# A 14-norm transformer kernel on one Trainium2 core: where a centred norm subtracts its mean, and where the square-root table is loaded

## The reference

```python
def rmsnorm(x, g):
    y = x * lax.rsqrt(jnp.mean(x * x, axis=-1, keepdims=True) + EPS)
    return y * g

def layer_norm(x, g, b):
    mu = jnp.mean(x, axis=-1, keepdims=True)
    var = jnp.mean(jnp.square(x - mu), axis=-1, keepdims=True)
    return (x - mu) * lax.rsqrt(var + LN_EPS) * g + b

# second block, each sublayer, latent and context alike
x = layer_norm(ALPHA * x + gate * y, ln_g, ln_b)
h = x * (1.0 + scale) + shift      # input of the next sublayer
```

## Time and profile before

| | |
|---|---|
| median of 3 runs | 2692.1 us (2691.15 to 2692.31) |
| profiled execution | 2694.41 us, its span 2692.6 us |
| TensorE, VectorE, ScalarE busy | 93%, 70%, 41% of the span |
| mean granted TensorE clock | 0.961 of full |
| table loads ahead of the square root (L1244) | 12, for 14 square roots |

### The profile page before, as it was taken

One profiled execution on the slowest core, in us unless ns is written; L12 is line 12 of the kernel. 1 busy time (PEld: TensorE's weight loads), 2 busy tenths in 40 slices (PEclk: granted clock), 3 DMA queues, 4 the chain that ended last, 5 costly groups with the idle time before them and its releaser, 6 DMA issues.

```text
span 2692.6 us, 39417 instructions
## 1 busy us (share of the span) xinstructions
PE 2494.2 (93%) x15494; PEld 2250.0 (84%) x15494; DVE 1889.5 (70%) x3654; ACT 1101.7 (41%) x1631; POOL 0.2 (0%) x4
## 2 busy tenths in 40 slices
PE   4998989789989998899999899999799999797997
PEld 3998889789979887688888798888798888676997
DVE  7877977788879975635555669887685344666666
ACT  3444564344453323624222562222552222545444
POOL 0000000000000000000000000000000000000000
PEclk8998999989989999999999899999899999798999
DMA  8875857768858752432322256666274332222553
GB/s 304 297 249 184 272 166 238 248 230 284 252 179 261 219 160 71 141 101 79 94 86 91 80 190 198 197 192 197 93 252 140 101 96 91 73 76 65 186 181 109
DMA packets 161096, 452.63 MB, mean 168 GB/s; under 512 B 17680, under 2 KB 21264, under 8 KB 160912
## 3 DMA queue, kind: packets, MB, share of 16 engines
q1 hardware_dynamic: 160912, 450.11, 51.7%
HBM read 448.99 MB, written 1.05 MB: 167 GB/s over the span
## 4 chain that ended last, share of the span: by engine, by line
PE 57%; DVE 7%; ACT 4%; issue 2%; DMA 0%; ACTq 0%; SPq 0%; DVEq 0%
PE PS L1012 18%; PE PS L1013 18%; PE PS L1014 18%; ACT whi L1221 2%; DVE wlo L1478 1%; DVE X L1578 1%; PE PS L1156 1%; DVE X L1576 1%; DVE RS L1545 1%; ACT NT L1275 1%; PE PS L1038 1%; ACT Uh L1271 0%; PE PS L1202 0%; PE PS L1040 0%; DVE X L1461 0%
## 5 line engine op out<-in xcount | busy, mean ns | idle before, releaser
L1478 DVE TENSOR_TENSOR wlo<-raw,whi 128x1024 fp32r<-128x1024 f32 x602 | 735.8, 1223 | 479.0 <-ACT whi L1221 476.2
L1012 PE MATMUL PS<-Uh,wlo 128*128 128x256 f32 (+1 forms) x2992 | 972.1, 325 | 66.6 <-DVE Ul L1582 30.5
L1013 PE MATMUL PS<-Ul,whi 128*128 128x256 f32 (+1 forms) x2992 | 954.2, 319 | 0.0
L1014 PE MATMUL PS<-Uh,whi 128*128 128x256 f32 (+1 forms) x2992 | 953.6, 319 | 0.0
L1221 ACT ACTIVATE whi<-raw 128x1024 fp32r<-128x1024 f32 x602 | 633.2, 1055 | 718.2 <-PE PS L1014 715.7
L1012 PEld LDWEIGHTS PS<-Uh,wlo 128*128 128x128 f32 x2992 | 581.6, 194 | 120.2 <-issue 45.2
L1013 PEld LDWEIGHTS PS<-Ul,whi 128*128 128x128 f32 x2992 | 584.0, 195 | 35.1 <-issue 0.2
L1014 PEld LDWEIGHTS PS<-Uh,whi 128*128 128x128 f32 x2992 | 583.3, 195 | 35.1
L1012 PE MATMUL PS<-Hh,wlo 128*128 128x256 f32 (+1 forms) x1616 | 519.2, 321 | 18.8 <-DVE RS L1548 10.5
L1013 PE MATMUL PS<-Hl,whi 128*128 128x256 f32 (+1 forms) x1616 | 514.7, 318 | 0.0
L1014 PE MATMUL PS<-Hh,whi 128*128 128x256 f32 (+1 forms) x1616 | 514.5, 318 | 0.0
(11 more groups left out here) (178 smaller groups left out, 1849.6 us busy)
## 6 DMA issues: line engine op xcount, KB each, us to landing
MODS<-in_mm SPq DMA_DIRECT2D x168, 256.0 KB, 3.8
SCR<-in_mm SPq DMA_DIRECT2D x168, 256.0 KB, 3.6
raw<-in_f0i SPq DMA_DIRECT2D x64, 512.0 KB, 4.0
raw<-in_f1i SPq DMA_DIRECT2D x56, 512.0 KB, 3.6
raw<-in_f2i SPq DMA_DIRECT2D x56, 512.0 KB, 3.6
SCR<-in_ma SPq DMA_DIRECT2D x88, 256.0 KB, 5.3
raw<-in_w1i SPq DMA_DIRECT2D x44, 512.0 KB, 4.4
raw<-in_w2i SPq DMA_DIRECT2D x44, 512.0 KB, 4.3
```

What stands on the lines that cost most here:

```text
L1012: e.matmul(o, ll, rh, start=start, stop=False)
L1013: e.matmul(o, lh, rl, start=False, stop=False)
L1014: return e.matmul(o, lh, rh, start=False, stop=stop)
L1478: e.tensor_tensor(wlo[:, w.n % RING, :], raw[:, w.n % RING, :], whi[:, w.n % RING, :].bitcast(F32), ALU.subtract).then_inc(s["wlo"].tell(w ...
```

## The change

1. `tally` puts one more item, `sqrt_table`: ACT takes the square root of one column of ones, in ACT's queue just ahead of the norm's first square. The compiler's load of the table moves there.
2. A centred norm subtracts the mean from X itself, before the scaling: `centre`, on two tiles at once, reads the sums in PSUM. The first pair's stands between `stat` and `root`; those of the other pairs stand behind the scaling of the pair before. The product L1548 and the subtraction L1578 go.
3. The sums' bank is held until the last `centre` instead of until `root`.
4. In the last norm the `centre` of pairs 2, 4 and 6 stand behind `root` and ahead of all eight scalings; each tile then has one DVE operation instead of two.

```diff
@@ tally
         self.tallies[r] = t
+        self.put("sqrt_table")
@@ tallied
         self.put("stat", n=t["n"], r=r, bank=t["bank"], centred=t["centred"], eps=eps)
+        if t["centred"]:
+            self.centre(t, 0)
         self.fill(min(fills[0] - 1, 1))
-        self.put("root", n=t["n"], r=r, bank=t["bank"], centred=t["centred"])
+        self.put("root", n=t["n"], r=r)
+        if not t["centred"]:
+            self.release(t)
+        self.fill(fills[0] - 2)
+        return t
+
+    def centre(self, t, k):
+        self.put("centre", n=t["n"], k=k, r=t["r"], bank=t["bank"])
+        if k == KT - 2:
+            self.release(t)
+
+    def release(self, t):
         b = t["bank"][0]
         self.held.discard(b)
         if self.turn % 8 == b:
             self.turn += 1
@@ norm_tiles
             self.put(what, st=site, k=k, n=t["n"], r=r, after=after, **fields)
+            if t["centred"] and k in (0, 2, 4):
+                self.centre(t, k + 2)
@@ schedule, the last norm
     t = p.tallied(LAT, 1e-5, (0, 0))
+    for k in (2, 4, 6):
+        p.centre(t, k)
@@ ACT
+                elif w.what == "sqrt_table":
+                    on.wait_ge(s["ones_set"], 0)
+                    e.activation(small[:, 216:217], ones[:, 0:1], ACT.Sqrt)
@@ DVE, root
                     e.reciprocal(rs, rs).then_inc(s["rstd"].tell(w.n), 1)
-                    if w.centred:
-                        on.wait_ge(s["rstd"], w.n)
-                        e.scalar_tensor_tensor(out=mr, in0=PS[:, b, 0:S], scalar=1.0 / D, in1=rs, op0=ALU.mult,
-                                               op1=ALU.mult).then_inc(s["mrs"].tell(w.n), 1)
-                        done_with(w.bank, "mrs", w.n)
+                elif w.what == "centre":
+                    x = X[:, w.k:w.k + 2, lo:hi]
+                    on.wait_ge(s["mean2"], w.n)
+                    e.scalar_tensor_tensor(out=x, in0=PS[:, b, 0:S].unsqueeze(1).broadcast_to([P, 2, S]), scalar=-1.0 / D,
+                                           in1=x, op0=ALU.mult, op1=ALU.add).then_inc(s["centred"].tell((w.n, w.k)), 1)
+                    done_with(w.bank, "centred", (w.n, w.k))
@@ DVE, the tiles
-                            on.wait_ge(s["mrs"], w.n)
-                            e.tensor_tensor(x, x, rs, ALU.mult).then_inc(s["normed"].tell((w.st, w.k, "x")), 1)
-                            on.wait_ge(s["normed"], (w.st, w.k, "x"))
-                            e.tensor_tensor(x, x, mr, ALU.subtract).then_inc(s["normed"].tell((w.st, w.k)), 1)
+                        if w.what == "ln":
+                            on.wait_ge(s["centred"], (w.n, w.k))
+                        on.wait_ge(s["rstd"], w.n)
+                        e.tensor_tensor(x, x, rs, ALU.mult).then_inc(s["normed"].tell((w.st, w.k)), 1)
@@ DVE, finish
-                    on.wait_ge(s["mrs"], w.n)
-                    e.tensor_tensor(x, x, RS[:, 0, 0, :], ALU.mult).then_inc(s["final_x"].tell((w.k, 0)), 1)
-                    on.wait_ge(s["final_x"], (w.k, 0))
-                    e.tensor_tensor(x, x, RS[:, 0, 1, :], ALU.subtract).then_inc(s["final_x"].tell((w.k, 1)), 1)
+                    on.wait_ge(s["centred"], (w.n, w.k - w.k % 2))
+                    on.wait_ge(s["rstd"], w.n)
+                    e.tensor_tensor(x, x, RS[:, 0, 0, :], ALU.mult).then_inc(s["final_x"].tell(w.k), 1)
```

More of the change, by code:

```diff
@@ L322, in tallied @@
             self.turn += 1
-        self.fill(fills[0] - 2)
-        return t
     def norm_tiles(self, what, site, t, r, fills, after, **fields):
@@ L818 @@
     "root2", "prob2", "turned2", "o_hi", "last_x",
-    "ones_set", "wlo", "modded", "coef", "folded", "var", "rstd", "mrs", "normed", "ulo", "product", "hlo", "acc", "angle", "padded",
+    "ones_set", "wlo", "modded", "coef", "folded", "var", "rstd", "centred", "normed", "ulo", "product", "hlo", "acc", "angle", "padded",
     "pooled", "roped1", "mapped", "y_lo", "masked", "weight1", "merged", "m_lo", "v_part", "v_stat", "v_normed", "mixed",
@@ L1426, in scalar @@
                     x = X[:, w.k, 0:S]
-                    on.wait_ge(s["final_x"], (w.k, 1))
+                    on.wait_ge(s["final_x"], w.k)
                     e.activation(x, x, ACT.Identity, scale=vec("lg", 40 + w.k), bias=vec("lb", 40 + w.k)).then_inc(
@@ L1541, in vector @@
                 elif w.what == "root":
-                    h = lo // S
-                    rs, mr = RS[:, h, 0, :], RS[:, h, 1, :]
+                    rs = RS[:, lo // S, 0, :]
                     on.wait_ge(s["std"], w.n)
                     e.reciprocal(rs, rs).then_inc(s["rstd"].tell(w.n), 1)
-                    if w.centred:
-                        on.wait_ge(s["rstd"], w.n)
-                        e.scalar_tensor_tensor(out=mr, in0=PS[:, b, 0:S], scalar=1.0 / D, in1=rs, op0=ALU.mult,
-                                               op1=ALU.mult).then_inc(s["mrs"].tell(w.n), 1)
-                        done_with(w.bank, "mrs", w.n)
+                elif w.what == "centre":
[4 more added lines that the diff above has]
+                    done_with(w.bank, "centred", (w.n, w.k))
                 elif w.what == "rms":
@@ L1569, in vector @@
                         x = X[:, w.k:w.k + 2, lo:hi]
[L1570 to L1574, removed]
-                            on.wait_ge(s["mrs"], w.n)
-                            e.tensor_tensor(x, x, rs, ALU.mult).then_inc(s["normed"].tell((w.st, w.k, "x")), 1)
-                            on.wait_ge(s["normed"], (w.st, w.k, "x"))
-                            e.tensor_tensor(x, x, mr, ALU.subtract).then_inc(s["normed"].tell((w.st, w.k)), 1)
+                        rs = RS[:, h, 0, :].unsqueeze(1).broadcast_to([P, 2, S])
+                        if w.what == "ln":
+                            on.wait_ge(s["centred"], (w.n, w.k))
+                        on.wait_ge(s["rstd"], w.n)
+                        e.tensor_tensor(x, x, rs, ALU.mult).then_inc(s["normed"].tell((w.st, w.k)), 1)
                     low = w.k if w.what == "ctxu" else w.k - 1
```

## The result

| | before | after |
|---|---|---|
| median, us | 2691.95 (4 runs, 2691.15 to 2692.31) | 2666.51 (4 runs, 2665.04 to 2667.89) |
| profiled execution, its span | 2694.41, 2692.6 | 2667.44, 2665.6 |
| mean granted clock | 0.961 | 0.963 |

The ratio is 0.9906 with an interval of 0.9894 to 0.9918: faster by 25.4 us, 0.94%. Forecast were 2673 and a range of 2665 to 2684.

What follows compares the result with a forecast made beforehand. TensorE, 93% busy, loses time to norms only where it waits on the ACT and DVE chain to the last `Ul`. Terms 4.6 + 0.9 + 2.5 + (2.5 + 3.3) + 3.8 + 1.7 = 19.3 us: 2692.1 to 2673, range 2665 to 2684.

Steps and rivals of the forecast that it cites:

- forecast: Whole kernel, likeliest case: the summed gains hold, 2667 to 2679 us; chance 0.62.
- more than forecast: Rival: a norm's low-clock stretch falls away or the last centre is nearer 0.68; up to 6 us more, 2667 or below; 0.08.
- The chain of l11: At l11, 1.61 up to the first `Uh` plus 2.16 over three pairs: 3.8 us, all on the path.
- The last norm: At the last norm, ACT's first tile comes later but tiles follow at 0.51 instead of 0.80: 1.7 us gained.
- The pair of the context norms: Context norms without the subtraction: pairs gain 0.72, 0.36, 0.36, 0.72; with 0.27, 2.5 us at c00, c02 and c10.
- The `mean2` of c01: At c01 the root behind the Silus loads the table again: `mean2` at 1504.8 instead of 1503.25.
- The bank's wait: The 10.5 us PE waits for L1548 lie ahead of a longer wait for the folded sums, so not worth 10.5.
- The table: A table load taken away is worth 0.49 us, not its 1.28; at c00 the gain is gone.
- l01 and l02 lie under twelve context tiles: nothing.: Latent norms l01 and l02: hidden under twelve context tiles, gain nothing.
- l00's cap: At l00, TensorE works through to a wait of only 1.21 at 1101.30: c00 and l00 give 4.6 us, not 5.8.
- the clock takes half of it: Rival: five more dense stretches at the low clock cost half their length, 10 us less gain, 2683; chance 0.17.
- c01: At c01 the second table load makes the reciprocal 1.7 late instead of 0.2; 0.9 us of gain is left.

Runs made afterwards that it cites:

- hold_only: Kernel before plus change 3 alone: the sums' banks of all ten centred norms held as long as in the change; 2691.58 us, ratio 1.0001.
- centre_only: Changed kernel without any early root; 2662.22 us, ratio 0.9894 to the kernel before.
- roots_only: Kernel before plus change 1 alone, the root of one column, norms as before; 2691.26 us, ratio 1.0002.
- centre_l01_l02: Kernel before with the mean taken first in norms l01 and l02 alone; 2688.19 us, ratio 0.9987.
- ctx_only: Kernel before with the mean taken first in context norms c00, c01, c02 and c10 alone, no roots; 2682.01 us, ratio 0.9968.
- after_again: The changed kernel, unaltered, timed once more in a later set; 2665.14 us, ratio 0.9901 to the kernel before.
- roots_late: Changed kernel with early roots only at l11 and the last norm, whose later centres each stand behind the scaling before; 2661.66 us, ratio 0.9888 to before.
- best2: roots_late with each context-norm centre right behind the accumulate of its fill's first tile; 2657.67 us, ratio 0.9874 to the kernel before.
- double: Changed kernel with a second DVE operation of the same size behind each centre; 2679.17 us, ratio 0.9955 to the kernel before.

## Why the prediction was right, and where it was off

**The number.** 2666.5 lies in the range of 2665 to 2684, by 1.5 us at its lower end. The case "forecast", 2667 to 2679 with 0.62, just missed it; it is the case "more than forecast", 2667 or below, that came true, and that had a chance of 0.08. That the number counts as right is partly luck: the sum was 19.3 us and the medians give 25.4.

**Right, by its own steps.** `centre` at 0.70 (684 ns). The chain of l11, 3.8 forecast and 3.58 measured; the first `Uh` 4.41 behind `mean2` instead of 2476.04 - 2469.91 = 6.13, so 1.72 earlier where 1.6 was forecast. The last norm, 1.7 and 1.59. The pair of the context norms: cycles of 5.70 and 5.99 after (1070.58 to 1076.57) against 6.36, where 6.0 was forecast, 2.5 a norm and 2.57 and 2.38 measured. The `mean2` of c01 at +1.5, 1.51 measured. l10's 3.3, 3.34. The bank's wait is nothing: shown by hold_only and by the folds' wait that took it over. The table: 0.49 where it isn't hidden, shown in l11, and hidden in the context norms, shown by centre_only. (By the 2.66 us for a switch that the Trainium skill gives in ScalarE: Activation LUTs, What ACT_TABLE_LOAD costs, roots_only would have gained some 1.9 at each of six norms, an estimate; the runs show 0.50 from `mean2` to the square root in l11 and nothing in the total. The load's 1283 ns agree, the drain isn't there.) One slip of counting: it is two of eight loads at centred norms that stay, not two of ten; L1264 has two after.

**The step that failed: "l01 and l02 lie under twelve context tiles: nothing."** It took for granted that TensorE, once it has the first tiles, is fed by the fill for as long as the norm lasts. Before, one pair of l01 takes 6.80 us on DVE, because two weight chunks pass through DVE and ACT in each:

```profile
1552.92 0.69 DVE L1576 TENSOR_TENSOR X<-X,RS 128x512 f32<-128x512 f32 x1
...
1556.44 1.23 DVE L1478 TENSOR_TENSOR wlo<-raw,whi 128x1024 fp32r<-128x1024 f32 x1 [1.77 <-ACT whi L1221]
...
1559.72 0.69 DVE L1576 TENSOR_TENSOR X<-X,RS 128x512 f32<-128x512 f32 x1
```

and TensorE has to wait for the first chunk of the pair that follows:

```profile
1564.52 0.39 PE L1012 MATMUL PS<-Uh,wlo 128*128 128x256 f32 x1 [0.78 <-DVE wlo L1478]
```

A second such wait follows in l01, 0.80, and l02 has two, 0.67 and 0.79. Such a wait costs more than it lists: the matmul ahead of it starts at 1563.46 and the one behind it at 1564.75, 1.29 for two steps that otherwise take 0.12 each, so 1.05 is lost. After, a pair takes 6.07 (scalings at 1544.12 and 1550.19), and no such wait is left. The count of matmuls (PE's busy time and, in brackets, their number) in the 30 us behind l01's `mean2` says the same: before, then centre_l01_l02. Behind l02's the counts are again 244 and 252, and hold_only has 244 behind l01's, so it isn't the bank.

```profile
1537.90:1567.90 30.00, 29.22 (x244) 29.01 (x243) 21.72 (x36) 22.39 (x37) 0.00 (x0) 1.00 0.39 125
```

```profile
1535.90:1565.90 30.00, 30.00 (x252) 30.00 (x251) 22.48 (x37) 25.70 (x43) 0.00 (x0) 1.00 0.44 141
```

So these norms were on the path, through `wlo` and not through `Ul`, and the weight chunks that queue behind the norm on DVE are what it held up. What they are worth can be read free of the clock if a part is ended where TensorE's own work begins or ends. From l01's `mean2` to the first matmul of the folded sums ahead of c02 it is 355.32 before, 355.33 in hold_only and 355.47 in ctx_only, but 353.27 in centre_l01_l02, 353.40 in centre_only and 353.26 after: 2.06, which is two waits of 1.05. From TensorE's first matmul of l02's fill to c10's `mean2` it is 356.53 before, 356.54 in hold_only and 356.53 in ctx_only, but 354.24 in centre_l01_l02 and 354.24 after: 2.29, two waits and a first matmul that ran at the low level before. So the norms that were put at nothing are worth some 4 us. (The 1.85 of l01 to c02 in the table is that 2.06 less 0.2: the work from the first of the sums to c02's `mean2` takes 5.68 before and 5.89 after, with a stretch at the low level in both, and 4.32 in hold_only and roots_only, where there is none.)

**l00's cap.** The 1.21 wait at 1101.30 made me stop l00's gain at 2.1; it is 3.40, all of the 3.3 that the same steps give without a cap. Between 1101 and 1116 the kernel before has four more waits of PE (0.33, 1.73, 1.09 and 0.64), for `wlo` and `Ul`; after, there are three in all of l00 (0.64, 1.10 and 1.13), none before 1105. So PE had room behind that wait too: the norm's chain set l00's length, and I had read one short wait as a limit without looking at those behind it.

**c02's 1.2 too much** is the rival "more than forecast", and so is the 0.9 that l02 to c10 gained beyond those 2.1. The granted clock at the end of c02's step, before, then ahead of that work in the changed kernel (PEclk is the third figure from the end):

```profile
1927.00:1934.00 7.00, 6.76 (x22) 5.48 (x23) 1.05 (x5) 5.26 (x11) 0.00 (x0) 0.53 0.09 36
```

```profile
1900.00:1912.00 12.00, 2.97 (x10) 2.61 (x11) 9.77 (x20) 7.74 (x15) 0.00 (x0) 0.57 0.30 87
```

Before, the low level, 1.2 GHz, still held while PE worked at the end of the norm; after, it falls on the stretch in which PE is idle (2.97 busy of 12) and is over when the work comes: from 1912 to 1921 the granted clock is 1.00. What that work takes at either level stands in the trace. The latent norm's sums are four pairs of matmuls that l02's `mean2` waits for; here are the first and the last pair, before, then after:

```profile
1929.89 1.05 PE L1038 MATMUL PS<-X,ones 128*128 128x256 f32 x2
...
1932.44 1.06 PE L1040 MATMUL PS<-SQ,ones 128*128 128x256 f32 x2
```

```profile
1917.58 0.59 PE L1055 MATMUL PS<-X,ones 128*128 128x256 f32 x2
...
1918.88 0.59 PE L1057 MATMUL PS<-SQ,ones 128*128 128x256 f32 x2
```

They take 3.61 us before and 1.89 after, 1.72 less. Before, `mean2` starts 0.04 behind them; after, it starts 0.96 behind them, because ACT is still at its Silu and that one's table load. So 0.80 of the 1.72 shows in c02 to l02. The other 0.92 shows in l02 to c10, where TensorE has begun the next sublayer 1.31 ahead of `mean2` (0.39 to 0.60 in the other traces). That part is 352.93 to 352.94 in the four traces (after, after_again, centre_only, roots_late) whose sums ran at the full clock, and 353.85 to 353.86 in the three whose sums took 2.71 to 2.86 (best2, double, centre_l01_l02).

The same reading for each context norm's step, with the length of the four pairs:

| step | sums before, after | less | less, without the sums' share | forecast |
|---|---|---|---|---|
| c00 to l00 | 1.88, 1.88 | 2.57 | 2.57 | 2.5 |
| Silus to l01 | 3.60, 3.21 | 1.45 | 1.06 | 0.9 |
| c02 to l02 | 3.61, 1.89 | 3.72 | 2.92 | 2.5 |
| c10 to l10 | 3.01, 3.31 | 2.38 | 2.68 | 2.5 |

The 0.4 that is left at c02 fits the output tiles just ahead of the sums, whose matmuls take 0.42 before and 0.28 after; that share is argued. centre_l01_l02, which doesn't centre c02, shortens c02's step all the same, by 0.75, with sums of 2.86. So the clock at the end of c02's step is shown as the cause of most of the excess, and the forecast of the chain was nearer than the first table says. Nothing in the forecast said that the low stretch would fall on idle time after; that part of the gain is luck.

In best2 the sums of c10 take 1.88 where roots_late has 2.94, which is 1.1 of its 2.3 there, and in the 20 us behind l11's `mean2` its granted clock is 0.57 where roots_late has 0.66.

Of the rival "the clock takes half of it" nothing came: it would have shown in hold_only, which has the idle time in one piece and took 1.0001. (The Trainium skill, TensorE: Matmul & The Clock Gate, Part 1, has the low level as the one that activity lifts; these rows agree, since it comes behind idle time and goes in work.)

**c01**: 1.45 instead of 0.9, and without the root 3.49 (Silus to l01 33.35 against 36.84), of which 0.93 are the sums (3.60 before, 2.67 in centre_only), so that 2.56 is left, as at c00. The root there was a loss, forecast as part of the 0.9 and not as something to leave out.

## What to carry to other kernels

An engine works its queue in order, so the price of an instruction is its neighbours: with the same `centre`, c00's step took 30.4, 29.3 or 28.4 us as it stood behind `wlo`, ahead of the accumulate, or just behind it. Put it where the engine idles for another engine, and behind what that other engine waits for. Before a stage is written off as hidden, compare its period with what the engine it feeds needs in that time, over all that passes through the same queue: l01's pair took 6.80 us with two weight chunks in it, and the chunks were what ran late. Before a difference of 1 us between two traces is explained, compare the granted clock and the time of the same matmuls at the ends of the part: four pairs took 1.9 us in one and 3.6 in the other. A load moved ahead is only gained where the engine idles at its new place: behind the Silus of c01 it cost 1.5 us.

## What the hardware showed that was not expected

A DVE operation with one operand in PSUM, read twice over by a broadcast, lasts 684 ns for 128x512, as long as one in SBUF alone (686). A reciprocal of half that size lasts 1747 ns. A table load of 1283 ns costs the square root behind it 0.50, since it is issued while ACT waits for DVE. One execution differs from the next by up to 4 us in the 1057 us ahead of the first centred norm, in kernels that are the same up to there, which is more than most of the single parts of this change.
